# Layers written out, down chunks bank by bank and activation operands in quarters, in a two-layer fp32 block

## The reference, cut to what matters

```
for l in range(2):
    x = x + 0.5 * swiglu(rms_norm(x, n1), gate1, up1, down1)   # FFN 1, width 2816
    h = rms_norm(x, nm);  z = h @ w_in                          # token mixing:
    ...  window attention, sliding attention, gates ...
    x = x + merged @ w_out
    x = x + 0.5 * swiglu(rms_norm(x, n2), gate2, up2, down2)   # FFN 2
swiglu(x) = (silu(x @ w_gate) * (x @ w_up)) @ w_down
```

## Time and profile before

| what | value |
|---|---|
| three runs | 3255.53, 3265.03, 3264.46 us; median 3264.46 |
| the profiled execution | 3264.27 us, its span 3262.5 us |
| TensorE | busy 2930.5 us, 90% of the span; mean granted clock 0.944 |
| VectorE, ScalarE, GpSimd | busy 1876.7, 1480.6, 846.8 us |
| stage 0, first gate and up matmul | 836.54 us |
| stage 0 to token mixing | 1204.88 to 1220.56 us |
| w_out to stage 1 | 1672.09 us |
| stage 1 to stage 2 | 2044.87 us |
| stage 2 to token mixing | 2417.18 to 2432.86 us |
| w_out to stage 3 | 2883.81 us |
| end of the last matmul | 3252.49 us |

### The profile page before, as it was taken

The page is one execution under the profiler, slowest core; times in us unless marked ns, Lnnn a source line. Parts: engine busy times, 40 slices in busy tenths (PEclk is TensorE's granted clock), DMA queues, the critical chain, the costliest instruction groups (busy, mean ns, idle before and its releaser), DMA issues.

```text
span 3262.5 us, 48404 instructions
## 1 busy us (share of the span) xinstructions
PE 2930.5 (90%) x16264; PEld 2460.3 (75%) x16264; DVE 1876.7 (58%) x2469; ACT 1480.6 (45%) x2173; POOL 846.8 (26%) x442
## 2 busy tenths in 40 slices
PE   4988869997799988989999999899988979989998
PEld 3755657775699866767779988799766767779987
DVE  7544268885788334662258852888234652268843
ACT  3251337774655333653245542655234643255532
POOL 2430201111122332113332224222432113322234
PEclk8997969998899998999999999999999989999999
DMA  6610249996133231101223222232231102223322
GB/s 273 263 39 1 90 166 357 369 363 238 52 103 103 84 123 65 39 32 64 90 78 104 103 84 97 80 107 98 84 129 52 39 26 77 84 86 104 105 85 104
DMA packets 95095, 378.52 MB, mean 116 GB/s; under 512 B 10816, under 2 KB 11088, under 8 KB 92624
## 3 DMA queue, kind: packets, MB, share of 16 engines
q1 hardware_dynamic: 88928, 349.74, 30.6%
q0 software_dynamic: 4608, 16.78, 1.3%
q10 hardware_dynamic: 1456, 10.66, 0.8%
HBM read 364.55 MB, written 16.78 MB: 117 GB/s over the span
## 4 chain that ended last, share of the span: by engine, by line
PE 46%; issue 36%; POOL 7%; DVE 5%; DMA 4%; ACT 2%; POOLq 0%; DVEq 0%; ACTq 0%; SPq 0%
PE pb L1421 8%; PE pb L1423 8%; PE pb L1422 8%; POOL w_lo L485 6%; PE pb L1102 6%; PE pb L1103 5%; PE pb L1104 5%; DMA rows<-h_rows,h_idx 3%; PE pb L1109 1%; PE pb L1175 1%; DVE rs L1676 1%; DVE g_wl L2078 1%; PE pb L1230 0%; PE pb L1229 0%; PE pb L1303 0%
## 5 line engine op out<-in xcount | busy, mean ns | idle before, releaser
L485 POOL TENSOR_TENSOR w_lo<-raw,w_hi 128x1024 fp32r<-128x1024 f32 x220 | 546.3, 2484 | 1302.7 <-ACT w_hi L566 1302.7
L1421 PE MATMUL pb<-bl,g_wh 128*128 128x256 f32 x2464 | 717.1, 291 | 54.5 <-DVE bl L2128 31.2
L1422 PE MATMUL pb<-bh,g_wl 128*128 128x256 f32 x2464 | 705.8, 286 | 0.0
L1423 PE MATMUL pb<-bh,g_wh 128*128 128x256 f32 x2464 | 705.7, 286 | 0.0
L1421 PEld LDWEIGHTS pb<-bl,g_wh 128*128 128x128 f32 x2464 | 481.0, 195 | 65.5 <-DVE bl L2128 33.4
L1422 PEld LDWEIGHTS pb<-bh,g_wl 128*128 128x128 f32 x2464 | 481.1, 195 | 4.8 <-issue 4.8
L1423 PEld LDWEIGHTS pb<-bh,g_wh 128*128 128x128 f32 x2464 | 480.6, 195 | 0.0
L566 ACT ACTIVATE w_hi<-raw 128x1024 fp32r<-128x1024 f32 x220 | 231.6, 1053 | 284.3 <-PE pb L1104 268.0
L1102 PE MATMUL pb<-hl,w_hi 128*128 128x512 f32 (+1 forms) x688 | 290.1, 422 | 51.7 <-DVE hl L1687 18.7
L1102 PE MATMUL pb<-fl,w_hi 128*128 (+1 forms) x704 | 280.5, 398 | 8.8 <-DVE fl L2168 8.8
L1103 PE MATMUL pb<-bl,w_lo 128*128 128x512 f32 x704 | 279.9, 398 | 0.0
(11 more groups left out here) (368 smaller groups left out, 5612.0 us busy)
## 6 DMA issues: line engine op xcount, KB each, us to landing
raw<-in_wstream SPq DMA_DIRECT2D x220, 512.0 KB, 3.3
m_raw<-in_moe_stream SPq DMA_DIRECT2D x192, 512.0 KB, 6.5
g_own<-in_gu_stream SPq DMA_DIRECT2D x45, 768.0 KB, 4.1
raw<-in_gu_stream SPq DMA_DIRECT2D x44, 768.0 KB, 4.1
ada_ring<-in_ada SPq DMA_DIRECT2D x8, 2048.0 KB, 8.1
g_own<-in_gu_stream SPq DMA_DIRECT2D x45, 256.0 KB, 2.5
hidf<-in_gu_stream SPq DMA_DIRECT2D x44, 256.0 KB, 2.6
adaw<-in_ada SPq DMA_DIRECT2D x4, 2048.0 KB, 23.0
```

The source lines that it names most:

```text
L485: pool.tensor_tensor(w_lo[s][:], raw[s][:], w_hi[s][:].bitcast(F32), ALU.subtract).then_inc(w_lod, 1)
L1421: pe.matmul(o, lh, rl, start=first and k == 0, stop=False, skip_group_check=True)
L1422: pe.matmul(o, ll, rh, start=False, stop=False, skip_group_check=True)
L1423: m = pe.matmul(o, lh, rh, start=False, stop=k == 3, skip_group_check=True)
```

## The change

Both layers are written out on each engine instead of looped over; `lvec` and its semaphore go, and the vectors are read from `lvec_all`. Then, around the seams:

- **Down, bank by bank.** Chunks 0 to 17 go as before. Chunks 18 to 21 are turned inside out: for bank 0 all four chunks, then bank 1, and so on, and each bank is released as it is full.
- **Six chunks split ahead.** Chunks 16 to 19 get high and low buffers of their own, in `bh` and in rows of `fl` that are free by then; 20 and 21 use `w_hi` and `w_lo`. Their splits wait for chunk 14 (21 for chunk 15) and no longer for the chunk two before.
- **Operands in quarters.** For stages 1 to 3 the operands are made in two-row pieces (`FINE`): the early ones (N11, T1) need x tiles 0 to 3 only and are made while the stage before still runs, so are the late ones of tiles 4 and 5 (with which 0 and 1 are combined); stage 0 keeps whole operands (`COARSE`). TensorE's first pair has another order: N11, T1, T2, 21, N3, N22, N4.
- **Sum of squares.** GpSimd adds the squares of x tiles 0 to 6 as they come (`add_squares`), and TensorE needs two `stat` matmuls, one for the sum and one for tile 7, instead of eight. Stage 2 sums four of them and has five matmuls; stage 0 keeps eight.
- **The reciprocal** for stages 1 to 3 comes ahead of pair 1's work on VectorE, not in the middle of it.
- **Output** in four transfers of two tiles each, instead of one.

```diff
+LATE, TAIL = NF - 6, NF - 4
+FINE = ((True, slice(0, 2)), (True, slice(2, 4)), (False, slice(0, 2)), (False, slice(2, 4)))
+COARSE = ((True, slice(0, 4)), (False, slice(0, 4)))
...
@@ sync
-            with sp.Fori(0, NL) as l:
+            for l in range(NL):
...
-            sp.wait_ge(x_ready, X_L + 3 * KD * NL)
-            sp.dma_start(out, x[:]).then_inc(out_done, 16)
+            for m in range(0, KD, 2):
+                sp.wait_ge(x_ready, X_L + 3 * KD * NL - KD + m + 2)
+                sp.dma_start(out[:, m:m + 2, :], x[:, m:m + 2, :]).then_inc(out_done, 16)
@@ gpsimd
+            def add_squares(n, j):
+                pool.wait_ge(sq_ready, 3 * KD + KD * n + j + 1)
+                if j > 1:
+                    pool.wait_ge(sq_sum, ADDS[n] + j - 1)
+                pool.tensor_tensor(rs[:], stemp[:] if j == 1 else rs[:], root_ring[j % 2], ALU.add).then_inc(sq_sum, 1)
...
+                    for k in range(LATE, NF):
+                        low_tail(b0, k)
+                    if h == 0:
+                        for j in range(1, KD - 1):
+                            add_squares(norm_of(f) + 1, j)
...
+                        for c in range(KD):
+                            low_one(wo + c)
+                            if c >= 3:
+                                add_squares(norm_of(f + 1), c - 2)
@@ scalar
+            def split_weight(b0, k):
+                act.wait_ge(w_raw[k % 2], 16 * (b0 + k // 2 + 1))
+                act.wait_ge(w_used, 2 * b0 + LATE - 1 + (k % 2 if k >= TAIL + 2 else 0))
+                act.activation(w_of(k)[0], raw[k % 2][:], ACT.Copy).then_inc(w_hid, 1)
...
+                for k in range(LATE, NF):
+                    f_split(k, k % 2)
+                    split_weight(b0, k)
...
-                his(lb + O_WO // 2, KD // 2 - 1)
-                first_pair(2 * NF * l + NF, NF * l + NF // 2)
+                for s in range(2):
+                    hi(wo + 1, s)
+                    take(f, s)
+                split_early(f, 0)
+                first_pair(Q0, n0)
+                for s in range(2):
+                    hi(wo + 2, s)
+                    take(f, 2 + s)
+                split_early(f, 1)
+                for s in range(2):
+                    hi(wo + 3, s)
+                    take(f, 4 + s)
+                split_late(f, 2)
@@ tensor
+                for m in range(KD):
+                    for k in range(TAIL, NF):
+                        if m == 0:
+                            pe.wait_ge(w_lod, 2 * bd + k + 1)
+                            pe.wait_ge(f_lo, NF * f + k + 1)
+                        to_hi, to_lo = w_of(k)
+                        ins = mm3(pb[m][:], to_hi[:, m, :], to_lo[:, m, :], f_hi_of(k, k % 2), fl[:, k, :], False, k == NF - 1)
...
+                    if m < KD - 1:
+                        ins.then_inc(bank_done, 1)
@@ vector
+                w_out_pair(0)
+                low_early(f, 0)
+                first_pair(Q0, n0)
+                w_out_pair(1)
+                low_early(f, 1)
+                w_out_pair(2)
+                low_late(f, 2)
+                w_out_pair(3)
```

More of the change, by code:

```diff
@@ L901, in ffn @@
-                hi_s31(Q0 + 1, n0, 1)
-                hi_s24(Q0 + 1)
-                for k in range(6, KD):
-                    square(q, k, root_ring)
-                Q1 = Q0 + 1
+                first, (gl, n) = (8, 10, 9), (len(groups(f)) - 1, norm_of(f))
+                if f == 0:
+                    for k in range(4):
+                        gained(f, k)
+                    split_early(f, 0)
+                    for k in range(4, KD):
+                        gained(f, k)
+                else:
+                    gained(f, KD - 1)
@@ new lines, in ffn @@
+                if f == 2:
+                    for k in range(4, KD):
+                        squared(f, k)
+                Q1 = Q0 + 1
+                hi_aa(Q1, n0, 1, 4)
+                if f == 0:
+                    for k in range(2, 6):
+                        squared(f, k)
+                hi_s31(Q1, n0, 1)
+                if f % 2:
+                    root_of_norm(n)
+                hi_s24(Q1)
+                if f == 0:
+                    squared(f, 6)
+                    squared(f, 7)
@@ L1411, in _, with stat_sum, stat_of, ffn @@
             stats(2, root_ring)
-            def ffn(f, Q0, b0, q, free):
-                def product(bank, w, b, first, ready=None):
-                    if ready is not None:
-                        pe.wait_ge(b_lo, 7 * f + ready)
+            def stat_sum(n):
+                pe.wait_ge(sq_sum, ADDS[n + 1])
+                pe.matmul(pb[0][:], ones, rs[:], start=True, stop=False, skip_group_check=True).then_inc(stat_mm, 1)
+            def stat_of(n, k):
+                pe.wait_ge(sq_ready, 3 * KD + KD * n + k + 1)
+                pe.matmul(pb[0][:], ones, square_to(n, k), start=SUMMED[n] == 0 and k == 0, stop=k == KD - 1,
+                          skip_group_check=True).then_inc(stat_mm, 1)
+            def ffn(f, Q0, b0, free):
+                def product(bank, w, b, first, name=None):
+                    if name is not None:
+                        pe.wait_ge(b_lo, PREP["lo", f, len(groups(f)) // 2 - 1 if name in ("N11", "T1") else len(groups(f)) - 1, name])
                     for k in range(4):
@@ L1467, in ffn, with down @@
                 bd = b0
-                def down(j, first, last):
+                def down(j, first):
                     for s in range(2):
```

481 lines of the change are left out of this document (325 added, 156 removed).

## The result

The changed kernel takes 3224.9 us, median of four runs (3220.38 to 3227.62), against 3264.7 for the kernel before: the ratio is 0.9882, 95% interval 0.9866 to 0.9897. The forecast was 3218 with a range of 3195 to 3244. Time and direction came out right, the make-up did not: the parts that I forecast give only -24.5 us instead of -45.8, and -25.6 came from something that the prediction does not contain.

A forecast was written before the change was run, and what follows sets the result against it. TensorE, busy 90% of the span, was taken as the bound, with time to win at the seams where it idles. Terms -13.4 + 10.0 - 22.7 - 10.7 - 3.7 - 5.3 = -45.8 gave 3218 us, range 3195 to 3244.

The forecast's parts named there:

- The norm's seam: Down product to token mixing, two seams: 9.0 us each instead of 15.7, 6.7 us less each, 13.4 less together.
- stage 2: Start of stage 2, behind stage 1's tail: 32.9 us against 43.6, 10.7 us less.
- chunk 4 of w_out: ScalarE's split of w_out chunk 4 comes late and TensorE waits: 3.5 us taken, bounds 0 and 6.
- The end: From the last matmul's end to the span's end: 4.7 us instead of 10.0, 5.3 us less.
- stage 0: Start of stage 0, keeping its pause in pair 2: 36.5 us against 40.2, 3.7 us less, bounds 0 and 7 less.
- the tail: Chunks 18 to 21 of the four down products: 2.5 us more each, 10.0 together, bounds 0 and 5 each.
- w_out and stages 1 and 3: From w_out to these stages' starts: 31.2 us against 44.0 and 41.1, 12.8 and 9.9 less, 22.7 together.
- The change adds or takes nothing inside these stretches: Steady gate and up pairs stay at 10.1 us, down product chunks at 5.6 us: no change.
- Clean hand-overs: Rival, all seams: nothing collides and reloads are quick, 21 us more gained, 3197 us; chance 0.18.
- Splits as the bound: Rival: tails lose 5 us each, w_out's chunk 4 6, starts have a second clock spell, 3243 us; chance 0.12.
- Lost time moving on: Rival: VectorE leaves pair 1 late, pairs 2 to 5 pay what starts save, 37 us, 3255 us; chance 0.05.
- Code loading: Rival: written-out layers need some 45 more instruction fetches, 67 us on top of the forecast, 3285 us; chance 0.05.

The follow-up runs named there:

- after_lvec_kept: The changed kernel with the removed 208-byte tile `lvec` put back unused, so all tiles lie where they lay before: 3247.3 us, ratio 0.9944.

## Why the prediction came out as it did

**Right, and by its own steps.** The norm's seam (9.0 against 9.06 us), stage 2 (32.9 against 33.5), chunk 4 of w_out (3.5 against 3.38), `up_hi` as what is late next, the absence of the 3.46 us pauses. The end took 3.8 us instead of 4.7, mainly because a 512 KB transfer out took 2.6, not the 3.2 of a load.

**Right by luck: stage 0 (36.5 against 36.1).** The prediction counts 1.7 us for lower clock behind the pause in pair 2. The pause is there (2.75 us), but in this execution the ten microseconds behind it ran at a granted clock of 1.00. In `after_lvec_kept`, with the same order in stage 0, they ran at 0.69. To the beginning of pair 4 the profiled execution took 56.7 us. Six profiles of kernels that begin stage 0 in the same order took 57.7, 58.2 and four times 60.5 to 60.6, where the kernel before and its variants took 60.1 to 60.3. So the forecast gain of 3.7 us comes in some executions and not in others.

**Wrong in size: the tail, "I take 2.5 ... with one collision".** It cost about 5.1 each, past the upper bound of 5 in three of four, which the prediction had named as a sign of being wrong. I priced the collision as an occasional addition to a chain of ScalarE, GpSimd and reloads. The runs show a different chain: VectorE's scaling takes 2.88 us beside back-to-back splits, and the weight split stands behind it on ScalarE. Loosening ScalarE's waits changed nothing, taking VectorE out of the chain (with one more buffer) gave 15 us.

**Wrong in size: w_out and stages 1 and 3.** "Two additions ... 1.8 us" was half the number: there are four, those of pair 2 included, and four pieces lost 4.3 us. Besides, in stage 1 the pauses of 3.06 and 2.30 each bring 3.4 us of half clock (from 1674.2 and from 1694.7), where I counted one such spell; and w_out's pause brings another (from 1643.5).

**Wrong in kind.** "The change adds or takes nothing inside these stretches" failed twice. Writing out the layers made the loads 0.5 us later, which a schedule without room for it (the low part begins as the addition does) turned into up to 0.3 us in about every second pair, 6.5 us. That was the other sign of being wrong, steady pairs over 10.1 us, and it came true. And the removed tile made 512-column matmuls 2.8% quicker. The last is decisive: with `lvec` kept the changed kernel takes 3247.3 us, outside my range. The forecast was met because errors of +21 and +8 us were met by one of -26.

**The rivals.** Clean hand-overs are out, every tail has a pause of 2.8 to 3.4 us in all. Splits as the bound is the one nearest to what the tails do. Lost time moving on did not happen at pairs 3 to 5 (they lose nothing that they had before but the 0.3 us). Code loading: writing out does cost time, 9 us and not 67, by another way.

On collisions the Trainium skill's "GPSIMD Engine Reference" (Specifications) was the rule to follow, with VectorE instructions that read two SBUF inputs: the ones stretched at these seams (0.68 to 1.75, 2.11 or 2.88 us) are all of that kind. The others bear it out. Beside GpSimd's work the additions to x with one input in PSUM keep their 0.69 us, and the reciprocal of one input its 3.35. But two inputs are not the only case: in token mixing the `SP<-SP,small` instruction (L2609), with one such tensor of 256 columns and a scalar per partition, goes from 0.35 to 2.44 us when it starts inside a GpSimd split, six times in the changed kernel's profile.

## What to carry to other kernels

- Cut the two spans at the same instructions and book every part, the untouched ones too. A total that agrees with a forecast proves none of its terms; here two unforeseen ones of 20 to 26 us cancelled.
- If a change removes or adds a tile, look at where the others moved, and try an unused pad before crediting the schedule. Look at both factors of a matmul, the weights too, not only at the one that moved.
- Before a part of a forecast is called right, compare it over several profiles: spells of lower clock alone moved one start by 3 to 4 us between executions with the same order.
- When a wait is removed and the pause stays, read its releaser again: two things may be late by the same time. And before moving a long operation out of one pause, ask whether the engine has room in the next pair.

## What the runs showed of the hardware

- A 512-column fp32 matmul of split operands follows the last after 227 ns when the addresses of its two factors leave the same remainder divided by 128 (0 and 0, or 96 and 96), and after 233 ns when they do not (96 and 0, 64 and 0, 32 and 96). That holds for all of them in four programs, the experts' `m_hi` included, and within one run for chunks 15 (233) and 16 (227). The 256-column ones take 120 ns in all four, but their factors `bl` or `bh` and `g_wh` or `g_wl` always leave the same remainder, so they are no test of it. Whether the number is 128 or 256, and why, is open.
- Loads of 256 KB land after 3.0 us or a little more in all eleven profiles of programs with written-out layers (3.0 to 3.2), wherever the tiles lie, and after 2.5 or 2.6 in the three with loops. The 768 KB loads differ less (4.1 to 4.3 against 4.0 to 4.1). The cause is open.
- A GpSimd addition holds a VectorE operation of two SBUF inputs until it ends, and is itself stretched (1.29 to 1.6 and 1.73 us). Beside GpSimd's splits of 2.55 us in a row, a 0.69 us operation took up to 2.88.
